# Copying the distance rows 128-fold in DRAM during the projection, and fetching the skewed bias per head into all 128 partitions

## The reference, cut to what matters

```python
def pattern_bias(rel_bias, dil, nk):
    dist = jnp.arange(nk + 1, dtype=jnp.int32) * dil
    return rel_bias[t5_bucket(dist)].astype(jnp.float32)
...
    bias = bias_k[jnp.minimum(jnp.maximum(dist, 0), nk)].transpose(2, 0, 1)
    s = jnp.einsum('bnqhd,bnkhd->bnhqk', qs, kb) + bias
```

## Time and profile before

| | us |
|---|---|
| median of 3 runs (1990.19 to 1990.63) | 1990.3 |
| the profiled execution | 1992.68 |
| its span, first to last instruction | 1991.1 |
| TensorE busy (matmuls) | 1741.2 (87%) |
| VectorE / ScalarE / GpSimd busy | 726.4 / 511.6 / 477.0 |
| mean granted TensorE clock | 0.936 of full |

### The profile page before, as it was taken

The page is one execution under the profiler, slowest core; times in us unless marked ns, Lnnn a source line. Parts: engine busy times, 40 slices in busy tenths (PEclk is TensorE's granted clock), DMA queues, the critical chain, the costliest instruction groups (busy, mean ns, idle before and its releaser), DMA issues. The chain is left out here.

```text
span 1991.1 us, 25066 instructions
## 1 busy us (share of the span) xinstructions
PE 1741.2 (87%) x9154; PEld 1512.0 (76%) x9154; DVE 726.4 (36%) x1065; ACT 511.6 (26%) x871; POOL 477.0 (24%) x455
## 2 busy tenths in 40 slices
PE   6889999966558888788869879999999999999994
PEld 5668888755436666677648679999999999999983
DVE  3200000068445666455434412323323333232326
ACT  4211111122124444565523321111111111111111
POOL 3200000066400000566505531111111111111106
PEclk9989999967768999999979989999999999999997
DMA  5476666334861100556433153333324324323315
GB/s 194 92 184 171 170 172 166 120 71 134 120 192 43 34 19 10 191 213 232 162 138 126 59 185 117 97 100 111 112 78 118 118 72 121 107 86 115 108 48 158
DMA packets 120277, 242.06 MB, mean 122 GB/s; under 512 B 19724, under 2 KB 81564, under 8 KB 115517
## 3 DMA queue, kind: packets, MB, share of 16 engines
q1 hardware_dynamic: 112288, 165.85, 26.4%
q0 software_dynamic: 6784, 71.32, 13.3%
q10 hardware_dynamic: 1152, 4.19, 1.7%
HBM read 210.58 MB, written 102.04 MB: 157 GB/s over the span
## 5 line engine op out<-in xcount | busy, mean ns | idle before, releaser
L427 PE MATMUL z_ps<-w_hi,h_hi 128*128 128x512 f32 x504 | 200.5, 398 | 21.1 <-POOL h_lo L300 11.6
L1909 POOL TENSOR_TENSOR f_lo<-f_t,f_hi 128x362 fp32r<-128x362 f32 (+1 forms) x66 | 61.0, 925 | 650.5 <-ACT f_hi L1960 650.5
L427 PE MATMUL z_ps<-w_lo,h_hi 128*128 128x512 f32 x504 | 199.0, 395 | 0.0
L427 PE MATMUL z_ps<-w_hi,h_lo 128*128 128x512 f32 x504 | 199.0, 395 | 0.0
L2073 PE MATMUL gate_ps<-h_hi,gu_hi 128*128 128x362 f32 (+1 forms) x528 | 173.3, 328 | 12.4 <-DVE gu_lo L2002 12.4
L2013 DVE TENSOR_TENSOR f_t<-s_t,up_ps 128x362 f32<-128x362 f32 (+1 forms) x66 | 35.1, 532 | 399.9 <-ACT s_t L1958 399.9
L1958 ACT ACTIVATE s_t<-gate_ps 128x362 f32<-128x362 f32 (+1 forms) x66 | 31.3, 474 | 574.7 <-PE up_ps L2073 574.7
L2021 DVE TENSOR_TENSOR acc<-acc,d_ps 128x512 f32<-128x512 f32 (+1 forms) x198 | 135.7, 687 | 117.6 <-PE d_ps L2084 117.5
L2073 PE MATMUL gate_ps<-h_hi,gu_lo 128*128 128x362 f32 (+1 forms) x528 | 173.6, 329 | 0.0
L2073 PE MATMUL gate_ps<-h_lo,gu_hi 128*128 128x362 f32 (+1 forms) x528 | 172.9, 327 | 0.0
L2073 PE MATMUL up_ps<-h_hi,gu_lo 128*128 128x362 f32 (+1 forms) x528 | 172.9, 327 | 0.0
(11 more groups left out here) (205 smaller groups left out, 3373.4 us busy)
## 6 DMA issues: line engine op xcount, KB each, us to landing
raw<-w_gu SPq DMA_DIRECT2D x88, 256.0 KB, 5.2
ks_sample<-cache_k_win POOLq DMA_DIRECT2D x60, 352.0 KB, 2.1
vs_sample<-cache_v_win POOLq DMA_DIRECT2D x60, 352.0 KB, 6.4
K<-cache_k_win SPq DMA_DIRECT2D x8, 2048.0 KB
V<-cache_v_win SPq DMA_DIRECT2D x16, 1024.0 KB, 4.9
w_raw<-w_in SPq DMA_DIRECT2D x14, 1024.0 KB
z_scratch<-z_out SPq DMA_DIRECT2D x56, 256.0 KB, 2.6
ks_sample<-cache_k_win POOLq DMA_DIRECT2D x18, 640.0 KB, 9.8
```

What stands on the lines that cost most here:

```text
L427: mm = pe.matmul(z_ps[t % 3][:, :], x[:, k, end - 128:end], w[:, par, k, :], start=(k, n) == first, stop=(k, n) == last)
L1909: pool.tensor_tensor(f_lo[cut], f_t[:, 0:n], f_hi[cut].bitcast(F32), ALU.subtract).then_inc(f_lo_ready, 1)
```

## The change

`tab` grows from 16 to 128 copies of each head's row. SP no longer writes the copies out of `row`: it stores the eight rows once to a new DRAM tensor `tab_row`. ACT, after the last evacuation of group 0, waits for that store and issues one DMA from DRAM to DRAM that reads `tab_row` 128 times and writes all of `tab` (4.72 MB). SP waits for both at the end of the projection. In the retention the bias is still fetched by eight DMAs at the same place in ACT's stream, but each now fills one head of `bias_p` in all 128 partitions.

```diff
-TAB_ROWS = 16
+TAB_ROWS = 128
...
                 sp.wait_ge(row_ready, 3)
-                sp.dma_start(tab, row[:, :].unsqueeze(1).broadcast_to([NH, TAB_ROWS, TABW])).then_inc(row_stored, 16)
+                sp.dma_start(tab_row, row[:, :]).then_inc(row_stored, 16)
                 ret.load_tabs(sp)
...
-                sp.wait_ge(row_stored, 16)
+                sp.wait_ge(row_stored, 32)
...
                 evacuate(0, TT - 1)
+                act.wait_ge(row_stored, 16)
+                act.dma_start(tab, tab_row.unsqueeze(1).broadcast_to([NH, TAB_ROWS, TABW])).then_inc(row_stored, 16)
                 with act.Fori(0, (GROUPS - 3) // 2) as i:
...
     def load_bias(self, eng):
-        for n in range(128 // TAB_ROWS):
-            eng.dma_start(self.bias_p[n * TAB_ROWS:(n + 1) * TAB_ROWS, :, :],
-                          bass.AP(tensor=self.tab.tensor, offset=127 - n * TAB_ROWS,
-                                  ap=[[TABW - 1, TAB_ROWS], [TAB_ROWS * TABW, NH], [1, SEQ]])).then_inc(self.bias_landed, 16)
+        for h in range(NH):
+            eng.dma_start(self.bias_p[:, h, :], bass.AP(tensor=self.tab.tensor, offset=h * TAB_ROWS * TABW + 127,
+                                                        ap=[[TABW - 1, 128], [1, SEQ]])).then_inc(self.bias_landed, 16)
 
     def finish(self, sp):
-        sp.wait_ge(self.bias_landed, 16 * 128 // TAB_ROWS)
+        sp.wait_ge(self.bias_landed, 16 * NH)
...
+    tab_row = scratch("tab_row_scratch", [NH, TABW])
```

More of the change, by code:

```diff
@@ L189, in load_vg, with in_projection @@
                       z[bass.ds(t * 128, rows), 2 * WID:4 * WID]).then_inc(self.vg_landed[par], 16)
-def in_projection(nc, A, z, h_hi, h_lo, ident, kept, tab, ret):
+def in_projection(nc, A, z, h_hi, h_lo, ident, kept, tab_row, tab, ret):
     GROUPS = ZC // WID
@@ L2130, in hymba_layer @@
                  nc.sbuf_tensor("h_lo", [128, KT, NTOK], F32R) as h_lo:
-                in_projection(nc, A, z, h_hi, h_lo, ident, kept, tab, ret)
+                in_projection(nc, A, z, h_hi, h_lo, ident, kept, tab_row, tab, ret)
         sems = lambda name, n: [nc.alloc_semaphore(f"{name}{i}") for i in range(n)]
```

## The result

The changed kernel takes 2000.6 us by the median of seven runs (1993.2 to 2003.5); the kernel before, run beside it, takes 1990.6 (1990.2 to 1994.5). The ratio of the runs is 1.004 (the two medians alone give 1.005), with a 95% interval of 1.0022 to 1.0058. It is slower by 10 us where a gain of 4.4 us was forecast, and outside the range of 1974 to 1997. The profiled execution is one of its quicker ones: 1996.97 us, span 1995.4.

A forecast was written before the change was run, and what follows sets the result against it. The prediction took TensorE, busy for 87% of the span, as the bound, with stalls in the retention and the projection's group 1. Retention -16.9 and projection +12.5 gave -4.4 us: 1990.3 to 1985.9 us, range 1974 to 1997.

The forecast's parts named there:

- The bias fetch: Retention: filling 128 partitions instead of 16 lifts the fetch from 114 to 410 GB/s; -16.9 us, from -14 to -19.
- Rival (c): Retention: odd source addresses limit the bias fetch, so it gets no faster; total +12, 2002 us; chance 0.06.
- The clock behind the restart: Retention: TensorE's first stretch after the zr wait runs at a higher clock; 0 to 2.2 us back, 1.1 taken.
- The wait on ACT: Projection, after group 0: ACT's wait for the row's store costs nothing, covered by some 8 us of slack.
- The copy's engines and rate: Projection: the copy runs on 8 engines, 128 rows each at 0.21 us a row, 27 us of eight engines.
- rival (b): Projection: the copy runs at the window copies' 13 GB/s, weights land at 152; total +10, 2000 us; chance 0.14.
- the rule named in the prediction: A DMA runs on the largest number of engines, up to 16, dividing both sides' slowest dimension: 8 for the copy.
- side estimate for 16 engines: Projection: were the copy spread over 16 engines, 64 rows and 13 us each, the loss would be about +3.
- The copy's delay of the weights: Projection, group 1: copy rows delay group 2's weights to 137, stall about 22 us; +12.5 us, from +3 to +18.
- 98 + 20.5 - 4 + 22 + 6 = 142: Weights' landing: queue start, tables and weights, gaps filled, 105 copy rows, GpSimd's next pair of window copies.
- the early case: Projection: the copy's first row comes at 100, so 105 rows pass before the weights, which land at 142.
- the old store's 3.4 us: Projection: without the old 16-fold store, tables and weights could start at about 98 instead of 101.4.

The follow-up runs named there:

- e21: The changed kernel with ACT issuing the copy as one block, first thing in the retention: 1980.7 us, beside 1988.2 for the kernel before.
- e22: The changed kernel with the copy first in the retention and no GpSimd window copies near the projection's group 1: 1979.4 us, beside 1988.2 before.
- e24: The changed kernel with the copy cut by head, one per prompt tile of the retention, and no window copies near group 1: 1966.7 us, beside 1988.1 before.
- e1: The changed kernel with the 128-fold copy kept but the bias fetched as before, 16 partitions at a time: 2014.9 us, beside 1987.8 before.
- e2: The changed kernel with each row stored once, no copy, and a 128-partition fetch from that row (another bias): 1969.5 us, beside 1987.8 before.
- e6: The changed kernel with the copy issued twice in a row, the second into another DRAM tensor: 2002.4 us, beside 1988.4 for the kernel before.
- e12: The changed kernel without the first three pairs of GpSimd's window copies, their bytes moved to the feed-forward network: 1980.2 us, beside 1988.4 before.
- e8: The changed kernel with the eleven table loads moved behind the last weights in SP's stream: 1981.1 us, beside 1988.2 for the kernel before.

## Why the prediction was wrong, point by point

**The bias fetch: the mechanism right, the gain somewhat too large.** Forecast -16.9 us (-14 to -19), measured -15.7 in the profiled execution. Over the fourteen kernels with a wide fetch (all but e21 and e22, where the block of the copy runs in the retention) the stage took 157.5 to 160.9 us, 159.4 on the mean; over the three with the old fetch 172.7. The gain is 13.3 us, just below the range. The rate was taken at 410 GB/s and is 372; `zr` lands in 5.9 us, not in 4; and the restart comes 15.5 us after ACT's first issue (547.62 - 532.14), where the forecast had 13.3 (522.1 - 508.81). In the kernel after that is due to the clock: from 532 to 545 us it was granted 0.50 (1.2 GHz), after TensorE had been busy for 2.3 of the 5 us before 530; the samples' table products took 4.77 us instead of 2.84, and they ended at the restart. In e24 they took 2.84 us, TensorE then waited 4.14 us for `zr`, and the restart came 15.3 us after the issue: there the load's own 6 us set it. The clock behind the restart gave 1.9 us (11.54 to 9.60), inside the bound of 0 to 2.2. Rival (c) is refuted by e1 and e2.

**The wait on ACT: right.** It cost nothing; its cover held.

**The copy's engines and rate: right.** 0.21 us a row over the whole copy, as forecast (0.19 in its first 3.5 us), so rival (b)'s mechanism, a slow row from 0.29 us on, did not come about. Its number, 2000 us, is the one measured, by luck. The sharing, packet by packet, shows again: 250 packets of the copy, on eight engines, beside 327 of SP's, where the earlier trace rows have 310 beside 311. For the number of engines the rule named in the prediction held too: laid out with 128 as the slowest dimension, the copy cost 11.4 us less (336.2 to 324.8). But the side estimate for 16 engines, a loss of about +3, was +13.7.

**The copy's delay of the weights: wrong, and this step turned the sign.** The forecast had the weights land at 137 and the stall grow to about 22 us. They were there at 148.4, and the stall was 36.0: +25.1 instead of +12.5. The row's store came 2.1 us earlier than the forecast had it, so on the forecast's clock the weights landed at 150.5, 13.5 us late. The step that failed is the sum for that landing, "98 + 20.5 - 4 + 22 + 6 = 142", and the choice of 137 below it. Its idea, turns packet by packet on eight engines, held; three of its terms were too small:

- 5 us by taking 137. That was a value between two cases, the copy's first row at 100 (142) or at 105 (128). The first row came at about 97.3, 99.4 on the forecast's clock, so the early case held. With 142 the forecast would have been no gain (+0.6 us) instead of -4.4.
- 4.2 us by the copy's rows: 127 of the 128 on each engine came in front of the weights, 26.2 us, not 105 in 22.
- 3.6 us by GpSimd's window copies: both pairs together kept an engine for 16.0 us, where the sum held 12.4 (6.4 for the first pair, inside the 20.5, and 6 for the second).

These make 149.8 beside the 150.5, and 150.5 + 10.3 - 134.8 = +26.0 beside the +25.1 measured: what follows the landing was right. That the pair behind the copy costs more than 6 us shows by itself in e6, where it comes late and the weights 10.1 us early.

At the worst stretch one sees what a turn is worth. At 122 to 130 us 13 window pieces held 0.549 x 16 x 8 / 13 = 5.4 us each, and only 11 rows of the copy ran, recorded at 1.3 us each instead of 0.2. At 130 us 572 packets of the copy were still to come before the weights landed. The Trainium skill ("DMA: Bandwidth & Descriptors", section "Queues, rings and completion order") says that an engine goes round its queues packet by packet and drains a whole packet before it turns to the next. The 310 beside 311 packets of the earlier trace rows agree; the views do not tell the engines apart, so one turn of a row to one window piece is not shown. Why a window piece slows from 3.35 to 4.0 us on the mean no run here shows either.

The window copies do a second thing: they hold SP's issues (5.88 us for the first table in e2, 6.37 in the kernel after, 0.35 without them). Taking the first three pairs away (e12) or the tables out of the queue (e8) each brings the weights back to 114 to 115 and takes 22 us off the stage.

**A term that was missed.** In e8 and e12, with the weights on time, the copy, with one pair of window copies beside it, still stalls TensorE by 13 to 14 us through the z stores of group 1; in e2, with the pair and no copy, the stall is 2.3. The forecast priced the copy only through the weights. It also took the old store's 3.4 us as a part of that sum; its removal is worth 8.5 us beside the window copies and nothing without them.

**The sum.** Span: +25.1 - 15.7 - 2.1 - 3.0 = +4.3. The medians differ by 10.0: the profiled execution of before lay 2.1 us above its median, that of after 3.6 below. Behind the retention everything together became 3.0 us shorter.

**Open.** The remedies don't add up: each of e8 and e12 takes off 22 us of 25. For the weights the estimate for e12 says why; how the 13 to 14 us that stay divide between the copy and the window pair beside it is not shown. The kernel after varied by 10 us from run to run (1993.2 to 2003.5); the kernel before varied by 4 beside it and by 10 in a later set of 22 runs (1982.6 to 1993.0), and why isn't settled for either. A fetch that needs no copies at all, with a falling skew out of one row, wasn't tried.

## What to carry to other kernels

A DMA between two DRAM tensors was not in the background here: price it by what is queued behind it on its engines, SP's next issues included, and by the other bulk copies that run then, not by its bytes against the idle share. If it must run beside loads that matter, cut it into pieces over all 16 engines (the two were tried together) and issue one with each step of a loop: the same 4.72 MB cost 33.6 us as one block at a full place, 13 us as one block at a place that looked free, and nothing that showed as eight pieces. A fetch into SBUF should fill all partitions; one into 16 ran at 114 GB/s, one into 128 at 372. And where a forecast has two cases, work out the total of each: with the weights at 142 the gain was already gone, and a value of 137 between the cases hid that.

## What the runs showed of the hardware

A DMA's issue can be held for many us beside bulk DMAs of another engine's queue: SP's issue took 13.69 us beside ACT's copy (e21), 19.79 us for the two issues of the weights beside both kinds of copies, and 0.35 us with neither (e12). It can be held by its own queue as well: ACT's issue of a second copy behind the first took 23.13 us (e6). A 40 KB piece of a window copy took 3.35 us on the mean in the kernel before and 4.0 us beside the copy of the rows, 5.4 us in the worst stretch. The projection's length, counted from a fixed step, repeated within 0.4 us between kernels that do not differ there, while the medians of whole runs moved by several us.
